# A hybrid decoder trunk: linear attention in unrolled turns of two blocks, and dense tiles with the column chunks as innermost loop

## What is computed

```python
def rmsnorm(x, g):
    y = x * lax.rsqrt(jnp.mean(x * x, -1, keepdims=True) + EPS)
    return y * g

def gla_chunked(q, k, v, glog, S0):          # chunks of C = 64 tokens
    def step(S, inp):
        qi, ki, vi, gi = inp
        G = jnp.cumsum(gi, axis=2)
        dec = jnp.exp(jnp.where(tri_incl, G[:, :, :, None, :] - G[:, :, None, :, :], -jnp.inf))
        attn = jnp.einsum('bhid,bhjd,bhijd->bhij', qi, ki, dec)
        o = (qi * jnp.exp(G)) @ S + attn @ vi
        gl = G[:, :, -1]
        S = S * jnp.exp(gl)[..., None] + jnp.einsum(
            'bhcd,bhce->bhde', ki * jnp.exp(gl[:, :, None] - G), vi)
        return S, o

x = x + odd_mixer(rmsnorm(x, norm_mix))      # projections, GLA, output projection
x = x + jnp.square(jax.nn.relu(rmsnorm(x, norm_mlp) @ mlp_w_up)) @ mlp_w_down
```

## Time and profile before

| | |
|---|---|
| median of 3 runs | 3421.15 us (3419.89 to 3435.81) |
| profiled execution | 3425.17 us, span of its instructions 3423.4 us |
| TensorE matmuls | 3016.1 us busy (88%), 19648 |
| TensorE weight loads | 2849.5 us busy (83%), 19648 |
| VectorE, ScalarE, GpSimd | 1158.2, 725.4, 241.3 us busy |
| mean granted TensorE clock | 0.890 of full speed |

### The profile page before, as it was taken

The page is one execution under the profiler, slowest core; times in us unless marked ns, Lnnn a source line. Parts: engine busy times, 40 slices in busy tenths (PEclk is TensorE's granted clock), DMA queues, the critical chain, the costliest instruction groups (busy, mean ns, idle before and its releaser), DMA issues. The chain is left out here.

```text
span 3423.4 us, 47095 instructions
## 1 busy us (share of the span) xinstructions
PE 3016.1 (88%) x19648; PEld 2849.5 (83%) x19648; DVE 1158.2 (34%) x1310; ACT 725.4 (21%) x975; POOL 241.3 (7%) x292
## 2 busy tenths in 40 slices
PE   6997799671489999999989996999778999999997
PEld 5997688560489999999979995777567999999996
DVE  5642432451342222222232125433344222222223
ACT  3211311250322121111221003111222202121213
POOL 1002222010010000000010003322001000000000
PEclk9998887685799999999999997666589999999998
DMA  4110000100211111111121110000321111111111
GB/s 132 44 49 24 2 2 2 54 2 21 78 37 42 45 43 49 43 45 47 43 86 43 49 38 7 1 0 0 105 80 31 49 44 49 43 49 43 46 46 49
DMA packets 222458, 142.21 MB, mean 42 GB/s; under 512 B 6418, under 2 KB 218721, under 8 KB 221860
## 3 DMA queue, kind: packets, MB, share of 16 engines
q1 hardware_dynamic: 222380, 141.08, 13.7%
HBM read 120.06 MB, written 21.10 MB: 41 GB/s over the span
## 5 line engine op out<-in xcount | busy, mean ns | idle before, releaser
L163 PE MATMUL ps<-act_hi,w_hi 128*128 128x344 f32 x3072 | 993.6, 323 | 101.1 <-DVE act_lo L381 51.5
L163 PE MATMUL ps<-act_lo,w_hi 128*128 128x344 f32 x3072 | 984.6, 321 | 0.0
L163 PE MATMUL ps<-act_hi,w_lo 128*128 128x344 f32 x3072 | 984.4, 320 | 0.0
L163 PEld LDWEIGHTS ps<-act_hi,w_hi 128*128 128x128 f32 x3072 | 579.9, 189 | 112.7 <-issue 85.0
L163 PEld LDWEIGHTS ps<-act_lo,w_hi 128*128 128x128 f32 x3072 | 580.1, 189 | 1.5 <-issue 0.7
L163 PEld LDWEIGHTS ps<-act_hi,w_lo 128*128 128x128 f32 x3072 | 580.2, 189 | 0.0
L163 PE MATMUL ps<-hidden_hi,w_hi 128*128 128x344 f32 x1536 | 493.5, 321 | 21.2 <-DVE hidden_lo L687 21.2
L163 PE MATMUL ps<-hidden_hi,w_lo 128*128 128x344 f32 x1536 | 491.8, 320 | 0.0
L163 PE MATMUL ps<-hidden_lo,w_hi 128*128 128x344 f32 x1536 | 491.3, 320 | 0.0
L143 ACT ACTIVATE w_hi<-w_raw 128x1024 fp32r<-128x1024 f32 x192 | 202.5, 1055 | 1194.3 <-PE ps L163 1144.0
L566 DVE TENSOR_TENSOR proj<-proj,ps 128x1032 f32 (+1 forms) x80 | 98.4, 1230 | 728.3 <-PE ps L163 728.3
(11 more groups left out here) (325 smaller groups left out, 2792.6 us busy)
## 6 DMA issues: line engine op xcount, KB each, us to landing
w_raw<-mlp_w_up SPq DMA_DIRECT2D x64, 512.0 KB, 4.1
w_raw<-mlp_w_down SPq DMA_DIRECT2D x64, 512.0 KB, 3.8
w_raw<-gla_w_in SPq DMA_DIRECT2D x24, 512.0 KB, 3.8
w_raw<-even_w_in SPq DMA_DIRECT2D x22, 512.0 KB, 3.8
x_save<-proj SPq DMA_DIRECT2D x2, 4128.0 KB, 12.2
proj<-x_save SPq DMA_DIRECT2D x2, 4128.0 KB, 12.3
x_rows<-x_prompt SPq DMA_DIRECT2D x8, 512.0 KB, 3.5
w_raw<-even_w_out SPq DMA_DIRECT2D x8, 512.0 KB, 4.2
```

What stands on the lines that cost most here:

```text
L163: last = c.nc.tensor.matmul(out, w[:, slot, k, :], x[:, k, cols], start=(k == 0 and n == 0), stop=(k == KT - 1 and n == 2))
```

## The change

Three things are changed. `multiply_tile` runs k outside, then the three products, then the column chunks, and calls `ready` before each k and with KT after the last. `level_masks` and `delta_masks` become one function, `chunk_masks`, which for GLA builds the masks 128 wide in passing memory and copies their two diagonal blocks to 64-wide ones, with a 64-wide identity. `gla_phase` is written out in four turns of two blocks: level products run chunk by chunk (64 by 64, on alternating halves of the output partitions), factors are made in place in a ring of three tiles straight from `proj`, without the copies of k and v and without the scaled q (the scale is now in ScalarE's copy of the output), and a turn's four chunk outputs go behind levels 0 to 3 of the next turn, with the eight state products first and then the eight attention products. Cut to its core:

```diff
@@ multiply_tile
-    for ch in range(NCH):
-        cols = slice(ch * CW, (ch + 1) * CW)
-        out = c.ps[:, 3 * slot + ch, 0:CW]
-        for k in range(KT):
-            if ready and (ch == 0 or (ch == 1 and k == 0)):
-                ready(k if ch == 0 else KT)
-            for n, (w, x) in enumerate(((c.w_hi, hi), (c.w_hi, lo), (c.w_lo, hi))):
-                last = c.nc.tensor.matmul(out, w[:, slot, k, :], x[:, k, cols],
+    for k in range(KT):
+        if ready:
+            ready(k)
+        for n, (w, x) in enumerate(((c.w_hi, hi), (c.w_hi, lo), (c.w_lo, hi))):
+            for ch in range(NCH):
+                last = c.nc.tensor.matmul(c.ps[:, 3 * slot + ch, 0:CW], w[:, slot, k, :],
+                                          x[:, k, ch * CW:(ch + 1) * CW],
                                           start=(k == 0 and n == 0), stop=(k == KT - 1 and n == 2))
+    if ready:
+        ready(KT)
     last.then_inc(c.tiles_done, 1)
@@ chunk_masks
+        do(g.memset(m[:], 0.0))
...
         for a in range(2):
             part = slice(a * CHUNK, (a + 1) * CHUNK)
             do(g.tensor_copy(lev[part], m[part, :, part]))
             do(g.tensor_copy(eye[part], c.ident[part, part]))
@@ gla_phase, ScalarE
+            for t in range(TURNS):
...
+                for x in range(NX):
+                    act.wait_ge(diffd, (2 * LEVELS + 1) * t + min(2 * x + 2, 2 * LEVELS + 1))
+                    a_(d[:, slot(t, x)], d[:, slot(t, x)], ACT.Exp, scale=1.0 / TAU).then_inc(expd, 1)
+                    if t and 1 <= x <= 4:
+                        o_cols(4 * (t - 1) + x - 1)
+                if t:
+                    act.wait_ge(od, 4 * t)
+                a_(qeg[:], logs[:, :, turn_tok(t)], ACT.Exp, scale=1.0 / TAU).then_inc(egd, 1)
+                for i in range(4):
+                    act.wait_ge(vturn, 4 * t + i + 1)
+                    a_(vn[:, i // 2, 4 * (i % 2):4 * (i % 2) + 4], B[VT[i % 2]], ACT.Copy).then_inc(vout, 1)
+                for b in range(2):
+                    act.wait_ge(kturn, 2 * t + b + 1)
+                    a_(kdn[:, b], B[KT_[b]], ACT.Copy).then_inc(kout, 1)
@@ gla_phase, TensorE
+            def product(t, y, left, right):
+                out = B[PROD[(NX * t + y) % 2]].rearrange("p (i n) -> p i n", i=SH)
+                if NX * t + y >= 2:
+                    pe.wait_ge(attd, NX * t + y - 1)
+                for b in range(2):
+                    for h in range(H):
+                        for a in range(2):
+                            last = m(out[half(a), b * H + h], left(h, b, a), right(h, b, a), start=True, stop=True)
+                last.then_inc(prodd, 1)
+
+            def chunk_out(n):
...
+                pe.wait_ge(stated, 1 + H * n)
+                if n:
+                    pe.wait_ge(oout, n)
+                o = B[OUT].rearrange("p (t n) -> p t n", t=2 * H)
+                for i in range(2 * H):
+                    m(o[:, i], state[:, i // 2, (i % 2) * P:(i % 2 + 1) * P], qeg[:, i // 2, chunk_in_turn(b, a)],
+                      start=i == 0, stop=False)
+                for i in range(2 * H):
+                    last = m(o[:, i], vn[half(a), b, i], att[half(a), t % 2, b * H + i // 2], start=False,
+                             stop=i == 2 * H - 1)
+                last.then_inc(od, 1)
                 for h in range(H):
+                    last = m(B[DS + h // 2][:, (h % 2) * GDV:(h % 2 + 1) * GDV], kdn[half(a), b, h],
+                             vn[half(a), b, 2 * h:2 * h + 2], start=True, stop=True)
                 last.then_inc(dsd, 1)
...
+            for t in range(TURNS):
+                product(t, 0, ...)
                 for level in range(LEVELS):
+                    w = d[:, slot(t, level)]
+                    pe.wait_ge(factd, (2 * LEVELS + 1) * t + 2 * level + 2)
+                    product(t, level + 1, ...)
+                    if t and level < 4:
+                        chunk_out(4 * (t - 1) + level)
...
+            for n in range(CHUNKS - 4, CHUNKS):
+                chunk_out(n)
@@ gla_phase, VectorE
                 for level in range(LEVELS):
+                    w_e, w_l = halves(d[:, slot(t, level)], level)
+                    dve.wait_ge(expd, NX * t + level + 1)
+                    v.tensor_tensor(w_e, w_e, halves(k, level)[0], ALU.mult).then_inc(factd, 1)
+                    v.tensor_tensor(w_l, w_l, halves(q, level)[1], ALU.mult).then_inc(factd, 1)
...
+                    else:
                         select(level - 1)
+                    if t and 1 <= level <= 4:
+                        new_state(4 * (t - 1) + level - 1)
```

More of the change, by code:

```diff
@@ L942, with chunk_masks @@
 BIG = -1e30
-def level_masks(c, area):
+def chunk_masks(c, area, delta):
     nc = c.nc
     made = c.sem(f"{area.name}_masks_made")
[L949 to L978, removed]
     lev = c.chunk_levels = area("chunk_levels", [P, LEVELS, CHUNK])
-    neg = c.chunk_bias = area("chunk_bias", [P, CHUNK])
     eye = c.chunk_eye = area("chunk_eye", [P, CHUNK])
-    sel = c.select = area("select", [8, 8, P])
-    brief = area.passing("delta_prepare")
+    if delta:
+        neg = c.chunk_bias = area("chunk_bias", [P, CHUNK])
+        sel = c.select = area("select", [8, 8, P])
+    brief = area.passing(f"{area.name}_prepare")
     m, wide = brief("levels_wide", [P, LEVELS, P]), brief("bias_wide", [P, P])
@@ L2134, in gla_phase @@
-    stored = s("stored")
+    (diffd, expd, factd, prodd, egd, egld, qegd, kturn, vturn, kout, vout, attd, od, oout, dsd, stated, stored) = map(s, (
+        "diff exp factors product q_decay chunk_decay q_decayed k_turned v_turned k_out v_out attention o o_out ds state "
+        "stored").split())
     SCALE = P ** -0.5
-    NX = LEVELS + 1
     B = [c.ps[:, n, :] for n in range(8)]
-    def halves(ap, level):
-        v = ap.rearrange("p h (b s) -> p h b s", s=2 * 2 ** level)
-        half = 2 ** level
-        return v[:, :, :, 0:half], v[:, :, :, half:]
@@ L2216, in _ @@
+            for n in range(CHUNKS - 4, CHUNKS):
+                o_cols(n)
         @block.tensor
         def _(pe):
[L2218 to L2234 removed]
@@ L2280, in _ @@
-            in_turns(pe, turn)
+            m = nc.tensor.matmul
+            def product(t, y, left, right):
[7 more added lines that the diff above has]
+                last.then_inc(prodd, 1)
@@ L2338, in turn @@
                 select(LEVELS - 1)
-            in_turns(dve, turn)
+            for n in range(CHUNKS - 4, CHUNKS):
+                new_state(n)
         @block.sync
         def _(sp):
-            sp.wait_ge(stated, 1 + 8 * NB)
+            sp.wait_ge(stated, 1 + H * CHUNKS)
             sp.dma_start(c.outs["p_state_gla"].rearrange("o b h k v -> k (o b h) v"), state[:]).then_inc(stored, 16)
```

298 lines of the change are left out of this document (120 added, 178 removed).

## The result

The changed kernel takes 3332.4 us (median of 4 runs, 3327.03 to 3337.17); the ratio to the kernel before on the same chip is 0.9727, with a 95% interval of 0.9687 to 0.9768; one of the four times of the kernel before, 3605.23 us, was taken in a slower state of the chip and is left out of it. The forecast was 3321, with a range of 3248 to 3362. The profiled execution has a span of 3335.4 us, 88.0 less than before.

A forecast was written before the change was run, and what follows sets the result against it. TensorE was taken to bound both the dense tiles and linear attention, the latter much of the time at its lower clock. Gains of 25 + 20 + 55 = 100 us from 3421.15 gave 3321, range 3248 to 3362.

The forecast's parts named there:

- dense spacing: Dense tiles: the new loop order leaves the 0.158 us matmul spacing unchanged, gain 0, bounds 28 us either way.
- down sections: First tile of each MLP down section: eight waits for the last hidden tile go, gain 25 us.
- norms: First tile behind each of four norms: the next tile starts 5.1 us earlier, gain 20 us, bounds 10 and 22.
- GLA: Linear-attention phase: 256 us where it took 311.6, gain 55 us, bounds 187 and 281.
- rivals 1 and 4: Dense tiles: equal weights loaded once, 3183 us, chance 0.03; or bank changes make the clock fall, 3666 us, chance 0.04.
- Rival 2: Linear attention keeps the upper clock level throughout: 187 us, not 256, so 3252 us in all; chance 0.11.
- a level takes about 2.5: First linear-attention turn: differences take 2.1 us a level with Exp and factors behind, about 2.5; the turn takes 28 us.
- VectorE is no bound: Linear attention: VectorE's instructions take some 23 us a turn, against 59 us forecast for the turn.
- One output and some of the turn's end at the upper level: Linear-attention turn: 3 us and 2 us come off the lower-level 64.6 us for these parts, leaving 59.
- 6 us for fetching unrolled code: Linear attention: an allowance for instruction fetch in the phase's upper bound of 281 us.
- 12.5 and 33 us of the lower bound: Linear attention at the upper clock: 12.5 us from a turn's last state product to the next output; last four chunks 33.
- the turn's 64.6 less 3 and 2: Linear-attention turn: 64.6 us at the lower clock, less 3 and 2 for parts at the upper level, taken as 59.

The follow-up runs named there:

- one-weight run: The changed kernel with w_hi in place of w_lo in the third product, so nine matmuls in a row share weights: 3320.92 us.
- run with full rows: The changed kernel with a chunk's attention and state products over all 128 rows, the other chunk's data included: 3277.53 us, GLA phase 206.7.
- alternating run: The changed kernel with a chunk's state and attention products alternating again, not eight and then eight: 3376.84 us, GLA phase 311.8.

## Why the forecast came out near

| step | forecast | measured |
|---|---|---|
| dense spacing | 0, bounds 28 either way | 6.5 us lost (11.333 to 11.367 us a tile) |
| down sections | 25 | 26.2 |
| norms | 20 | 22.6, of which 3.4 given back |
| GLA | 55 | 49.3 |
| sum | 100 | 88.2; the spans differ by 88.0 |

- **Dense spacing.** That equal weights are loaded again held (one-weight run), and the clock held in the tiles (99 of the 13824 matmuls start at the lower level, 81 before), so rivals 1 and 4 are out. The reading of starts to 0.01 us could not show the half nanosecond; it lies well inside the bound.
- **Down sections.** Right in mechanism and size: before, the eight tiles with the wait took 116.9 us from start to start, where eight undisturbed ones take 90.7. The run with only the norm's tile changed keeps all eight waits.
- **Norms.** From the last low part to the next tile 4.7 us where 4.8 was worked out; gains 6.9, 5.3, 5.2, 5.2. The first is larger since that norm had lagged before (11.6 us). The step that was missing is what comes after: the first input projection is bound by VectorE's convolution for some tiles, and takes 3.4 back (measured in the run with the norm's tile alone).
- **GLA.** A chunk 10.73 (10.7 worked out), the gap 1.9 (1.9), three turns 180.6 (177), the last four chunks and the end 49.9 (51.4), the first turn 31.7 (28). The first turn is the mis-sized term: "a level takes about 2.5" has GpSimd's two differences at 1.05 each and VectorE's work hidden behind them, with factors at 0.69. Beside each other both are slower: a difference takes 1.04 us alone and about 1.5 there, the second factor 1.52, and a level 2.95. Part of the same price stands in the waits at the turns' ends, which are shorter with GpSimd idle. "VectorE is no bound" holds for the turns and fails for the first.
- **The clock.** "One output and some of the turn's end at the upper level" came out as 6.8 to 10.2 us a turn. Rival 2 was priced right in its way (the run with full rows comes to 206.7 where 187 was the end), but its reason for staying away was wrong: not waits for loads (TensorE was busy for 10.73 us of the 10.73 us chunk), but products over 64 of the 128 rows.
- **What the sum hid.** It gave 55 us to a rewritten phase as a whole. The alternating run shows that without one edit in it, the grouping, nothing of the gain is left. The rest takes work from VectorE, ScalarE and GpSimd and gains nothing by it; the mean clock of the phase was 0.54 in that run, against 0.65 before. Why it is lower is open: the level products became 64 columns wide where they were 128, but they keep all 128 rows, so the run with full rows says nothing on them, and no run put the wide products back.
- **Terms without a row.** The 6 us for fetching unrolled code in the upper bound is shown by no run: in the changed phase TensorE has 0.9 us of idle time that ends on nothing the profile shows. The 12.5 and 33 us of the lower bound are not worked out, and the turn's 64.6 less 3 and 2 is 59.6, not 59. "Most of TensorE's waiting" beside the largest group is 101.1 us of 407 without a matmul. None of this moves the forecast by more than 2 us.
- **Luck.** That the parts add up to within 0.2 us of the spans is in part chance, since phases with the same code differ by 3 us and more between profiles.

## What to carry to other kernels

Read the granted clock of a phase before counting its instructions: filling a half-used contraction with zeros cost copies and gained 40 us in 262, since the clock doubled in the products. Look at several profiles of the same code before a gain is put down to the clock: here the upper stretch at a turn's end lasted 6.8 or 10.2 us without any edit. Undo each part of a rewrite alone; here undoing one line of grouping took back the whole gain of the phase. And when a start moves forward, look at which engine bounds the stretch behind it, as it may hand the time back.

## What the hardware showed that was not expected

- Chunk outputs with two of three parts over 64 rows ran at the lower clock although TensorE never idled (10.73 us busy in a 10.73 us chunk); with all parts over 128 rows, zeros included, the same stream got the upper level (5.50).
- TensorE changed its PSUM bank with every dense matmul for 623 us at a clock of 1.00. The Trainium skill ("TensorE: Matmul & The Clock Gate", "A second HAM failure mode: psum-queue depth-cycling") tells of a kernel whose clock swung with such cycling; this trace shows no drop.
- The order of three nested loops over equal matmuls moves their spacing between 156.7 and 157.9 ns; neither the number of bank changes nor that of weight changes puts the orders in line.
- Crossing between products of 128 and of 64 rows costs about 0.19 us a product at the lower clock (0.62 against 0.43).
- A VectorE product of two tiles took 0.68 us with GpSimd idle, and 1.52 (median) with GpSimd's differences beside it.
